# Moving the gathers of ten token chunks between the first expert products of a decoder layer

## The reference

```python
def hier_moe(h, wg_r, bg_r, we_r, be_r, w_gate, w_up, w_down):   # 4 groups x 8 experts
    ...                                    # router: each token gets 2 of 32 experts and weights
    y = jnp.zeros_like(hf)
    for grp in range(N_GROUPS):
        sl = slice(grp * EXPERTS_PER_GROUP, (grp + 1) * EXPERTS_PER_GROUP)
        hid = (jax.nn.silu(jnp.einsum("nd,edf->nef", hf, w_gate[sl]))
               * jnp.einsum("nd,edf->nef", hf, w_up[sl]))
        y = y + jnp.einsum("nef,efd->nd", hid * combine[:, sl, None], w_down[sl])
    return y.reshape(B, T, D)
```

## Time and profile before

| | |
|---|---|
| median of 3 runs | 1504.18 us (1502.48 to 1507.22) |
| profiled execution, span of its records | 1500.7 us (its own device time is not on the page) |
| PE busy | 1441.7 us, 96% of the span |
| DVE, ACT, POOL busy | 728.9, 508.2, 138.9 us |
| moved by DMA | 351.01 MB, mean 234 GB/s |
| share of the chain that ended last | PE 90%, DMA 4%, DVE 2%, issue 2%, ACT 1% |

### The profile page before, as it was taken

How to read it: one execution, slowest core, us unless ns; L and a number is a source line. 1 busy time by engine, 2 the same in 40 slices (tenths; PEclk the granted TensorE clock), 3 DMA queues, 4 the chain that set the end, 5 groups by cost and what they waited for, 6 DMA issues and landing times.

```text
span 1500.7 us, 27556 instructions
## 1 busy us (share of the span) xinstructions
PE 1441.7 (96%) x11917; PEld 1099.9 (73%) x11917; DVE 728.9 (49%) x1286; ACT 508.2 (34%) x876; POOL 138.9 (9%) x267
## 2 busy tenths in 40 slices
PE   7999999999999999999999999999999999989996
PEld 7998989989899999998879997875333333333332
DVE  4583946648347554555455334554333233223325
ACT  5543434325246454554444334432110110101003
POOL 7010010201110000000000000011212011110100
PEclk9999999999999999999999999999999999999998
DMA  8551332524275454445655515686999999999995
GB/s 247 170 169 59 121 115 69 166 66 153 74 233 181 152 169 138 144 159 181 222 168 168 169 55 186 230 340 249 379 421 421 421 421 421 421 421 422 421 412 220
DMA packets 161359, 351.01 MB, mean 234 GB/s; under 512 B 13824, under 2 KB 111706, under 8 KB 138330
## 3 DMA queue, kind: packets, MB, share of 16 engines
q1 hardware_dynamic: 161242, 349.30, 63.1%
HBM read 347.18 MB, written 2.10 MB: 233 GB/s over the span
## 4 chain that ended last, share of the span: by engine, by line
PE 90%; DMA 4%; DVE 2%; issue 2%; ACT 1%; SPq 0%; POOL 0%; DVEq 0%; POOLq 0%; ACTq 0%
PE banks L906 23%; PE banks L1439 14%; PE banks L1279 11%; PE banks L899 8%; PE banks L1475 7%; PE banks L1299 6%; PE banks L1517 4%; DMA expert_unit<-in_moe_w_down_dram 4%; PE banks L1067 1%; PE banks L926 1%; PE banks L1410 1%; PE banks L1324 1%; PE banks L1347 1%; PE banks L1050 1%; PE banks L1242 1%
## 5 line engine op out<-in xcount | busy, mean ns | idle before, releaser
L1439 PE MATMUL banks<-expert_unit,pair_entries 128*64 128x512 f32 x1024 | 242.7, 619 | 21.9 <-issue 21.1
L906 PE MATMUL banks<-hidden_lo_chunks,piece 128*128 128x256 f32 x928 | 263.3, 284 | 0.0
L1701 ACT CAST piece<-arena_fixed 128x1024 fp32r<-128x1024 f32 (+1 forms) x158 | 161.4, 1034 | 189.0 <-PE banks L906 148.1
L2129 DVE TENSOR_TENSOR piece<-arena_fixed,piece 128x1024 fp32r<-128x1024 f32 (+1 forms) x158 | 188.6, 1217 | 55.9 <-ACT piece L1701 55.4
L1439 PEld LDWEIGHTS banks<-expert_unit,pair_entries 128*64 128x64 f32 x1024 | 73.4, 141 | 162.5 <-issue 162.5
L906 PE MATMUL banks<-hidden_hi_low_chunks,piece 128*128 128x256 f32 x928 | 180.6, 293 | 0.0
L906 PE MATMUL banks<-hidden_hi_high_chunks,piece 128*128 128x256 f32 x928 | 179.3, 291 | 0.6 <-DVE hidden_lo_chunks L2112 0.6
L906 PEld LDWEIGHTS banks<-hidden_lo_chunks,piece 128*128 128x128 f32 x928 | 178.6, 192 | 0.0
L2395 DVE TENSOR_TENSOR loop_split<-arena_fixed,loop_split 128x2048 fp32r<-128x2048 f32 x48 | 107.9, 2288 | 110.8 <-ACT loop_split L1865 110.8
L906 PEld LDWEIGHTS banks<-hidden_hi_low_chunks,piece 128*128 128x128 f32 x928 | 145.3, 193 | 7.0 <-issue 3.8
L906 PEld LDWEIGHTS banks<-hidden_hi_high_chunks,piece 128*128 128x128 f32 x928 | 144.5, 192 | 7.1 <-issue 3.3
(11 more groups left out here) (406 smaller groups left out, 2079.1 us busy)
## 6 DMA issues: line engine op xcount, KB each, us to landing
expert_unit<-in_moe_w_gate_dram SPq DMA_DIRECT2D x60, 1024.0 KB, 22.5
expert_unit<-in_moe_w_up_dram SPq DMA_DIRECT2D x60, 1024.0 KB, 24.8
expert_unit<-in_moe_w_down_dram SPq DMA_DIRECT2D x52, 1024.0 KB, 22.4
arena_fixed<-in_w_in_dram SPq DMA_DIRECT2D x22, 2048.0 KB, 9.0
arena_fixed<-in_wk_mem_dram SPq DMA_DIRECT2D x8, 2048.0 KB, 9.1
arena_fixed<-in_wv_mem_dram SPq DMA_DIRECT2D x8, 2048.0 KB, 8.0
arena_fixed<-in_w_out_dram SPq DMA_DIRECT2D x8, 2048.0 KB, 8.0
arena_fixed<-in_wq_mem_dram SPq DMA_DIRECT2D x8, 2048.0 KB, 8.0
```

What stands on the lines that cost most here:

```text
L906: mm = pe.matmul(b[:, half * T:half * T + T], w(w_)[:, k % 8, :], hidden_x(x_, c), start=c + t == 0 and n > 0, stop=c == NC - 1 and t == 2 ...
L1439: mm = pe.matmul(bank[b][o, :].rearrange("p (g n) -> p g n", g=2), hs_pair[:, c, o], gate_up_unit(i(e))[:, :, c % (NC // 2), :], start=c = ...
L1701: nc.scalar.copy(piece_half(p, 0), raw_piece(p)).then_inc(piece_hi, 1)
L2129: V.tensor_tensor(piece_half(p, 1), raw_piece(p), piece_half(p, 0).bitcast(F32), ALU.subtract)\
```

## The change

The list of calls on PE is changed, and nothing else. Before, eight chunks are gathered ahead of the two quarters (0,0) and (0,1), then two chunks, then pair 1's first half, then six chunks, then the quarter (0,2). Now the quarter (0,0) follows six chunks, chunks 6 and 7 stand between (0,0) and (0,1), and chunks 14 and 15 stand between (0,2) and `pair_slots(0)`, which is ahead of (0,3).

```diff
             for c in range(4):
                 gather(c, (1,))
-            for c in range(4, 8):
+            for c in range(4, 6):
                 gather(c)
             gate_up(0, 0)
+            for c in range(6, 8):
+                gather(c)
             gate_up(0, 1)
-            gather(8)
-            gather(9)
+            for c in range(8, 10):
+                gather(c)
             gate_up(1, 0)
             gate_up(1, 1)
-            for c in range(10, NC):
+            for c in range(10, 14):
                 gather(c)
             gate_up(0, 2)
+            for c in range(14, NC):
+                gather(c)
             pair_slots(0)
             gate_up(0, 3)
             pair_slots(1)
```

## The result

The changed kernel takes 1507.69 us (median of 11 runs, 1505.26 to 1512.76) against 1504.36 us for the kernel before in the same comparison (11 runs). The ratio is 1.0021, with a 95% interval of 1.0011 to 1.0031: it is slower by 3.2 us (1.7 to 4.7). That is less than 0.3%, and still the interval excludes no change; the prediction had held that so small a difference can't be told. The forecast was 1507.8 us: three idle times (3.3 us) and two more changes between gathers and products, 3.6 us together.

A forecast was written before the change was run, and what follows sets the result against it. PE sets the pace until the load at 1063.71 us, the full-rate weight stream afterwards. Three idle times (3.3 us) plus two more gather/product changes make 3.6 us, added to 1504.18 for 1507.8 us; range 1503.2 to 1511.2, 8 times in 10.

The forecast's parts named there:

- the load behind (1,3): SP's load issued when PE ends quarter (1,3), at 1063.71 us before; forecast at 1067.3, the end 3.6 us later.
- three idle times: PE waiting ahead of quarters (0,0), (0,1) and (0,3): 0.8, 1.5 and 1.0 us, 3.3 us together.
- two more changes between gathers and products: PE switching between the two kinds of matmul; the rest of the 3.6 us beside 3.3 us of idle times.
- one hole: DMA engines run dry just ahead of 1063.71 us, waiting for PE; forecast to be 3.6 us longer.
- Step 1: Quarter (0,0): PE idle 0.8 us behind DVE's copy, start at 1023.80 us, 1.00 us early.
- Step 2: Quarter (0,1): PE idle 1.5 us behind ACT's copy, start at 1030.91 us, 2.6 us late.
- Step 3: Quarter (0,2): no wait, by a margin of 0.2 us; start 0.7 us late.
- Step 4: Quarter (0,3): PE idle 1.0 us behind ACT's copy, start at 1054.4 us, 3.6 us late.
- POOL's handover of 0.14 us: The one such wait in the chain, taken as the time from a copy's end to PE's first product.
- Rival A: PE's clock falls in the new pauses; one slow quarter gives 1509.5 us, all three 1512.9 us; chance 0.15.
- Rival B: The stream depends on its first load, issued 1.0 us earlier at (0,0)'s end; end 1.0 us earlier, 1503.2 us; chance 0.06.
- Rival C: The stream has slack behind 1063.7 us and takes up PE's lateness; no change, 1504.2 us; chance 0.14.

The follow-up runs named there:

- the six without halves: The profiled kernels other than those in which SP issues two more pairs of units in halves; the change among them has ratio 1.0021.
- e6: Against the kernel before, four extra matmuls nobody reads, in front of the down product of pair 1 at about 1083 us; 1503.87 us, ratio 0.9991.
- e1: Against the kernel before, only chunks 6 and 7 are moved behind the quarter (0,0); ratio 1.0025.
- e3: Against the kernel before, six chunks ahead of (0,0), four between (0,0) and (0,1), two ahead of (1,0), four ahead of (0,2); ratio 1.0016.

## Why the prediction was right

**The place.** The prediction said that PE's lateness at the load behind (1,3) reaches the end one to one, because the stream is dry at that point and full afterwards. The eight experiments and the change give nine pairs of numbers; in the six without halves, load and stream agree within 0.2 us, whether the lateness came from a wait, from added matmuls or from a slow clock. e6 shows the other side: 3.68 us behind that point cost nothing. The picture of how it happens was too simple: the prediction put all the lateness into one hole that grows by 3.6 us, and that hole grew by 1.1 us, the rest being lost in gaps between the half-unit loads ahead of it. In e1, whose load was 2.71 us late, the stretches from 1034 to 1038 have shares of 0.60 and 0.83. The sum holds because it depends on the load behind (1,3) alone.

**The terms.** Step 1 was 0.8 us of idle time, measured 0.77. Step 2 was 1.5, measured 1.39. Step 3 was no wait, by a margin of 0.2 us, and there was none. Step 4 was 1.0, measured 0.83. The three were each a little too high, 3.3 in sum against 2.99, because I had taken POOL's handover of 0.14 us for ACT's and DVE's: in the chain of the changed kernel ACT's copy ends at 1055.55 and PE starts at 1055.59.

```profile
1055.45 0.10 ACT pair_entries L1989
1055.55 0.04 issue
1055.59 3.68 PE banks L1439 x16
```

The changes between gathers and products were too low, 0.3 against 0.67: a quarter that is followed by a gather took 3.59 us from start to start (1024.93 to 1028.52), not 3.51. The two errors of 0.3 us cancel, and the sum of 3.6 stands at 3.66. One reading was off without harm: the 0.14 us behind POOL is the handover alone. PE idled 0.87 us there, before and after the change alike.

**The rivals.** Rival A, a clock that falls in the new pauses, did not happen. In the changed kernel the stretch from 1024 to 1062 has a granted clock of 1.00, and the quarters behind 0.77, 1.39 and 0.83 us of idle time all took 3.65 us. The rule of the Trainium skill that spoke for it (TensorE: Matmul & The Clock Gate, A second HAM failure mode: psum-queue depth-cycling) doesn't show here for pauses of this size. Rival B had the stream depend on its first load. In e1 that load went out 10.19 us after the first gather, 0.98 us earlier than before, and the kernel is slower. (In the profile of the change the slow clock hides it: 11.44 us, against 11.17 before.) What was won there was lost again in the gap before the next half-unit load, not only at 1063 as the prediction had it. Rival C, slack in the stream, would have shown as a late load without a late stream, and none of the six kernels without halves has that.

**What was luck.** The span of the profiled execution grew by 3.6 us, as forecast, but out of 3.66 for the waits, 1.3 for a slow clock at the gathers and about the same back at the last wait. The medians over 11 runs, 3.3 us apart, don't rest on that one execution. Luck as well is that the handovers and the changes were off by the same 0.3 us in opposite directions.

## What to carry to other kernels

Where a kernel goes from compute-bound to a stream at full rate, find the last point at which the stream has nothing left to move. In this kernel time lost ahead of it was lost at the end, and 3.7 us lost behind it cost nothing. Don't expect the loss to show in that hole alone: count the MB moved. Work put ahead of a consumer covers a handover only as long as it is longer than the way through the other engines; here two gathers (2.1 us) didn't cover 3.5 us of gather, scaling and copy, and four (3.96 us) did. Bound what closing a hole can give by the idle share inside it, before anything else.

## What was not expected of the hardware

- The gathers ran at a granted clock of about 0.5 for their first 2 to 3 us in three of the ten profiles (the change, e3 and e6), and at 1.00 in the others, with the same instructions ahead of them. In these three the eight small matmuls just ahead were slow already (1.34 to 1.42 us instead of 1.19). It cost 1.3 us in the gathers each time.
- Behind the long waits for weights late in the kernel, the same idle time gave either level. In the profile of the changed kernel:

```profile
1231.45 5.35 PE L1439 MATMUL banks<-expert_unit,pair_entries 128*64 128x512 f32 x16 [2.70 <-issue]
1261.46 3.65 PE L1439 MATMUL banks<-expert_unit,pair_entries 128*64 128x512 f32 x16 [1.93 <-issue]
```

  and 2.73 us at 1441.68 left the clock high, shown above. Over the ten profiles 89 quarters stand behind such waits. The 22 behind less than 1.97 us all took 3.65 us; of the 67 behind 1.97 to 2.83 us, 34 took 5.00 us or more and 33 took 3.65.
- Half loads of the down matrices (512 KB each) took the full share of the DMA engines at a lower rate than the 1 MB loads of the kernel before in that stretch (407 against 424 GB/s). Whether it is the size of the load or of its contiguous runs, no run here shows.
